# Cache attention: where the halves of the score rows are added, on VectorE or on TensorE

## What is computed

```python
qf = q.astype(jnp.float32) * (HEAD_DIM ** -0.5)
for k, _, kp in segs:
    s = jnp.einsum('bthjd,bshjd->bhjts', qf, k.astype(jnp.float32))
    dist = (q_pos[:, None] - kp[None, :]).astype(jnp.float32)
    s = jnp.where(dist >= 0, s - slopes[None, :, None, None, None] * dist, NEG_INF)
    scores.append(s)
p = jax.nn.softmax(jnp.concatenate(scores, axis=-1), axis=-1)
a = p[:, :, 0] - lam * p[:, :, 1]
...
    out = out + jnp.einsum('bhts,bshe->bthe', a[..., off:off + n], v.astype(jnp.float32))
```

## Time and profile before

| | |
|---|---|
| median of 3 runs | 3715.0 us (3714.81 to 3717.43) |
| span of the profiled execution | 3713.6 us |
| PE busy | 3481.8 us, 94% |
| DVE busy | 1857.9 us, 50% |
| ACT busy | 1495.0 us, 40% |
| POOL busy | 609.4 us, 16%, none of it before slice 6 of the 40 |
| first stage of the key pages | about 470 to 558 us |
| seven passes | 568 to 1349 us |

### The profile page before, as it was taken

One profiled execution on the slowest core, in us unless ns is written; L12 is line 12 of the kernel. 1 busy time (PEld: TensorE's weight loads), 2 busy tenths in 40 slices (PEclk: granted clock), 3 DMA queues, 4 the chain that ended last, 5 costly groups with the idle time before them and its releaser, 6 DMA issues.

```text
span 3713.6 us, 65939 instructions
## 1 busy us (share of the span) xinstructions
PE 3481.8 (94%) x24423; PEld 3386.7 (91%) x24423; DVE 1857.9 (50%) x2599; ACT 1495.0 (40%) x2255; POOL 609.4 (16%) x489
## 2 busy tenths in 40 slices
PE   5999979999999987899999999999889999999997
PEld 5999978888898885789999999999889999999997
DVE  4333366666666677454444444444564444444444
ACT  3232147777777775333222222222333333333223
POOL 0000007777777740000000000000000000000000
PEclk8999999999999998799999999999999999999998
DMA  4344357777887781234444444444334444444442
GB/s 144 124 154 134 128 176 290 292 292 292 303 315 292 292 305 61 68 125 136 140 144 137 143 141 137 148 137 144 120 102 149 158 141 156 148 148 148 148 150 71
DMA packets 337733, 634.25 MB, mean 171 GB/s; under 512 B 10056, under 2 KB 255919, under 8 KB 303151
## 3 DMA queue, kind: packets, MB, share of 16 engines
q1 hardware_dynamic: 335042, 616.60, 47.9%
q0 software_dynamic: 2192, 14.25, 1.2%
q10 hardware_dynamic: 348, 1.07, 0.1%
HBM read 623.11 MB, written 9.23 MB: 170 GB/s over the span
## 4 chain that ended last, share of the span: by engine, by line
PE 89%; DVE 5%; issue 2%; ACT 2%; DMA 0%; POOL 0%; DVEq 0%; ACTq 0%; POOLq 0%
PE ps L1436 66%; PE ps L1542 6%; PE ps L1530 6%; PE ps L1557 5%; PE ps L1568 2%; DVE halves L1055 1%; PE ps L1572 1%; ACT halves L666 1%; PE ps L1797 1%; ACT halves L696 1%; DVE parts L928 0%; PE ps L1696 0%; DMA io_tm<-in_x_sample_dram 0%; DVE xf L954 0%; DVE halves L1066 0%
## 5 line engine op out<-in xcount | busy, mean ns | idle before, releaser
L1436 PE MATMUL ps<-xhi,halves 128*128 128x336 f32 (+1 forms) x6784 | 1551.7, 314 | 28.4 <-DVE xlo L960 14.4
L901 DVE TENSOR_TENSOR halves<-raw,halves 128x2048 fp32r<-128x2048 f32 x328 | 751.8, 2292 | 1000.5 <-ACT halves L605 1000.5
L1436 PEld LDWEIGHTS ps<-xhi,halves 128*128 128x128 f32 x6784 | 1156.7, 189 | 32.6 <-issue 32.5
L605 ACT ACTIVATE halves<-raw 128x2048 fp32r<-128x2048 f32 x331 | 633.8, 1915 | 1200.1 <-PE ps L1436 1186.0
L1436 PE MATMUL ps<-xlo,halves 128*128 128x336 f32 (+1 forms) x3392 | 1066.7, 314 | 0.0
L1436 PEld LDWEIGHTS ps<-xlo,halves 128*128 128x128 f32 x3392 | 642.1, 189 | 0.0
L545 POOL TENSOR_TENSOR halves<-raw,halves 128x512 fp32r<-128x512 f32 x452 | 575.1, 1311 | 313.2 <-ACT halves L696 313.1
L1055 DVE TENSOR_TENSOR halves<-ps,halves 128x512 fp32r<-128x512 f32 x512 | 341.5, 688 | 194.2 <-ACT halves L666 194.1
L666 ACT ACTIVATE halves<-ps 128x512 fp32r<-128x512 f32 x512 | 292.1, 594 | 225.7 <-PE ps L1530 225.4
L1436 PE MATMUL ps<-hA_hi,halves 128*128 128x336 f32 (+1 forms) x1408 | 374.8, 313 | 4.9 <-DVE hB_lo L1328 4.9
L1436 PE MATMUL ps<-hB_hi,halves 128*128 128x336 f32 (+1 forms) x1408 | 373.7, 312 | 0.0
(11 more groups left out here) (178 smaller groups left out, 2796.1 us busy)
## 6 DMA issues: line engine op xcount, KB each, us to landing
raw<-in_w_gate_up_dram SPq DMA_DIRECT2D x176, 1024.0 KB, 5.1
raw<-in_cache_k_dram SPq DMA_DIRECT2D x128, 1024.0 KB, 4.8
raw<-in_cache_v_dram SPq DMA_DIRECT2D x128, 1024.0 KB, 4.9
raw<-in_w_down_dram SPq DMA_DIRECT2D x88, 1024.0 KB, 5.0
raw<-in_w_qkv_dram SPq DMA_DIRECT2D x48, 1024.0 KB, 5.1
raw<-in_w_o_dram SPq DMA_DIRECT2D x16, 1024.0 KB, 5.7
out_dram<-kv_tm POOLq DMA_DIRECT2D x4, 1024.0 KB, 5.4
raw<-in_w_pool_dram SPq DMA_DIRECT2D x4, 1024.0 KB, 5.1
```

The costliest lines, as they stand in the source:

```text
L605: act.activation(whi[t][:, :], raw[r][:, :], ACT.Copy).then_inc(hi_ready[t], 1)
L901: dve.tensor_tensor(wlo[t][:, :], raw[r][:, :], whi[t][:, :].bitcast(F32), ALU.subtract)\
L1436: mm = pe.matmul(out, l, r, start=first and n == 0, stop=last and n == 2)
```

## The change

The fold matmuls go. `turn_bank` becomes `turn_probs`, which transposes probabilities only. `raw_scores` becomes four reductions on VectorE over 64 partitions each, two that stay in their half and two that read one half and write the other, so that `s_raw[:, 0, :]` and `s_raw[:, 1, :]` hold the two rows of each score. For that the two parts of the queries change places for g = 1 (`qp_at`). `scores_out` adds the bias to the first and then the second to it, both in SBUF, with a wait on VectorE's own semaphore between (`score_bias`), and does not wait for ScalarE any more. Bank 3 is used less often, and so its counts change.

```diff
@@ def qp_at
-            at = 8 * P * g + TS * half_
+            at = 8 * P * g + TS * ((half_ + g) % 2)
@@ VectorE
                 two = ps[2][:, :].rearrange("p (g a k) -> p g k a", g=2, a=2)
-                dve.tensor_reduce(s_raw[:, :, :], two, AX.X, ALU.add).then_inc(bank_free[2], 1)
-
-            def scores_out(p, fill, last):
-
-                dve.wait_ge(bank_full[3], before("cache", 3, True) + fill + 1)
-                ins = dve.scalar_tensor_tensor(out=sc[:, bass.ds(PAGE * p, PAGE)], in0=alibi,
-                                               scalar=pagestep[:, bass.ds(p, 1)], in1=ps[3][:, P:P + PAGE],
-                                               op0=ALU.add, op1=ALU.add)
-                ins.then_inc(bank_free[3] if last else score_step, 1)
+                halves_ = (slice(0, TS), slice(TS, P))
+                for g in range(2):
+                    dve.tensor_reduce(s_raw[halves_[g], 0, :], two[halves_[g], g], AX.X, ALU.add)\
+                        .then_inc(score_parts, 1)
+                dve.tensor_reduce(s_raw[halves_[0], 1, :], two[halves_[1], 0], AX.X, ALU.add).then_inc(score_parts, 1)
+                dve.tensor_reduce(s_raw[halves_[1], 1, :], two[halves_[0], 1], AX.X, ALU.add).then_inc(bank_free[2], 1)
+
+            def scores_out(p, page):
+
+                dve.wait_ge(score_parts, 3 * page + 3)
+                dve.wait_ge(bank_free[2], bank_n("cache", 2, 0) + page + 1)
+                dve.scalar_tensor_tensor(out=s_raw[:, 0, :], in0=alibi, scalar=pagestep[:, bass.ds(p, 1)],
+                                         in1=s_raw[:, 0, :], op0=ALU.add, op1=ALU.add).then_inc(score_bias, 1)
+                dve.wait_ge(score_bias, page + 1)
+                dve.tensor_tensor(sc[:, bass.ds(PAGE * p, PAGE)], s_raw[:, 0, :], s_raw[:, 1, :], ALU.add)\
+                    .then_inc(score_step, 1)
@@ VectorE, step of a pass
                         if v == 1 or not first:
-                            dve.wait_ge(a_hi, (NPAGE + 1) * s + m + 2)
-                            scores_out(m - 1, CF0 + CFS * s + m + 1, False)
+                            scores_out(m - 1, NPAGE + NPAGE * s + m - 1)
@@ TensorE
-            def turn_bank(fill, page, count, slot):
-
+            def turn_probs(fill, count, slot):
 
                 pe.wait_ge(bank_free[3], before("cache", 3, False) + fill + 1)
-                if page is not None:
-                    pe.wait_ge(bank_free[2], bank_n("cache", 2, 0) + page + 1)
-                    for g in range(2):
-                        mm = pe.matmul(ps[3][:, P:2 * P], fold[:, TS * (1 - g):TS * (1 - g) + P], s_raw[:, g, :],
-                                       start=(g == 0), stop=(g == 1))
-                if count is not None:
-                    pe.wait_ge(staged, count)
-                    mm = pe.matmul(ps[3][:, 0:H * NT], stage[slot][:, :], comb, start=True, stop=True)
-                mm.then_inc(bank_full[3], 1)
+                pe.wait_ge(staged, count)
+                pe.matmul(ps[3][:, 0:H * NT], stage[slot][:, :], comb, start=True, stop=True).then_inc(bank_full[3], 1)
+
+            def scores_free(page):
+
+                pe.wait_ge(score_parts, 3 * page)
+                pe.wait_ge(bank_free[2], bank_n("cache", 2, 0) + page)
```

More of the change, by code:

```diff
@@ L69 @@
 U_END = U_F1 + 12 * BLOCKS
-CF0, CFS = NPAGE, NPAGE + 2
+CF0, CFS = 0, NPAGE + 1
 FREE_USES = [
@@ L336, in trunk @@
         v_hi, v_part, v_used = map(sem, ("v_hi", "v_part", "v_used"))
+        score_parts, score_bias = map(sem, ("score_parts", "score_bias"))
         best_step, smax, sexp, csum, score_step, c_ready, staged, a_hi, anew_ready, dve_step = map(
@@ L1096, in _ @@
                     if j > 0:
-                        scores_out(4 * i + j - 1, 4 * i + j - 1, True)
-                        dve.wait_ge(bank_free[3], bank_n("cache", 3, j) + 4 * i)
+                        scores_out(4 * i + j - 1, 4 * i + j - 1)
+                        dve.wait_ge(score_step, 4 * i + j)
                         best_of(4 * i + j, 4 * i + j - 1)
                 raw_scores(U_C0 + 3, i, 4)
-                scores_out(4 * i + 3, 4 * i + 3, True)
-                dve.wait_ge(bank_free[3], bank_n("cache", 3, 4) + 4 * i)
+                scores_out(4 * i + 3, 4 * i + 3)
+                dve.wait_ge(score_step, 4 * i + 4)
                 best_of(4 * i + 4, 4 * i + 3)
@@ L1115, in softmax @@
                 dve.wait_ge(best_step, NPAGE + 1 + (NPAGE - 1) * s)
-                dve.wait_ge(bank_free[3], bank_n("cache", 3, CF0 - 1) + 1 + CFS * s)
+                dve.wait_ge(score_step, NPAGE + NPAGE * s)
                 dve.tensor_reduce(mx, sc[:, LASTP:], AX.X, ALU.max).then_inc(csum, 1)
@@ L1144, in new_part @@
                 dve.wait_ge(anew_ready, s + 1)
-            dve.wait_ge(bank_free[3], bank_n("cache", 3, CF0 - 1) + 1)
             new_scores(0)
@@ L1177, in _ @@
                 raw_scores(U_CM + 3, s * (NPAGE // 2) + NPAGE // 2 - 1, 4)
-                scores_out(NPAGE - 1, CF0 + CFS * s + NPAGE + 1, True)
+                scores_out(NPAGE - 1, NPAGE + NPAGE * s + NPAGE - 1)
                 softmax(s + 1)
@@ L1590, in _ @@
                     turn(p, U_C0 + j, 2, i, 4)
-                    if j > 0:
-                        turn_bank(p - 1, p - 1, None, 0)
-                    else:
-                        pe.wait_ge(bank_free[2], bank_n("cache", 2, 0) + p)
-                    turn(p, U_C0 + j, 3, i, 4)
+                    turn(p, U_C0 + j, 3, i, 4)
+                    if j == 0:
+                        pe.wait_ge(bank_free[2], bank_n("cache", 2, 0) + p)
+                    else:
+                        scores_free(p)
                     for g in range(4):
@@ L1599, in _ @@
                             turn(p + 1, U_C0 + j + 1, g - 2, i, 4)
-                turn_bank(p, p, None, 0)
             A1 = NPAGE + 1
@@ L1605, in _ @@
                     turn(NPAGE + NPAGE * s, U_CM + 1, g, s * (NPAGE // 2), 4)
-                turn_bank(CF0 + CFS * s, None, A1 * s + 1, 0)
+                turn_probs(CF0 + CFS * s, A1 * s + 1, 0)
                 def two_steps(i):
@@ L1625, in two_steps @@
                         skip = first and v == 0
-                        turn_bank(CF0 + CFS * s + m + 1, None if skip else page - 1, A1 * s + m + 2, (v + 1) % 2)
+                        turn_probs(CF0 + CFS * s + m + 1, A1 * s + m + 2, (v + 1) % 2)
+                        scores_free(page)
                         if skip:
@@ L1634, in _ @@
                     two_steps(i)
-                turn_bank(CF0 + CFS * s + NPAGE + 1, NPAGE * (s + 2) - 1, None, 0)
             s = NB - 1
-            turn_bank(CF0 + CFS * s, None, A1 * s + 1, 0)
+            turn_probs(CF0 + CFS * s, A1 * s + 1, 0)
             with pe.Fori(0, NPAGE // 4) as i:
@@ L1641, in _ @@
                     pe.wait_ge(bank_free[3], B3 + CF0 + CFS * s + m + 2)
-                    turn_bank(CF0 + CFS * s + m + 1, None, A1 * s + m + 2, (v + 1) % 2)
+                    turn_probs(CF0 + CFS * s + m + 1, A1 * s + m + 2, (v + 1) % 2)
                     for g in range(4):
```

2 lines of the change are left out of this document (1 added, 1 removed).

## The result

The changed kernel takes 3871.2 us, median of 4 runs (3869.81 to 3875.15), beside 3715.2 of the kernel before on the same chip: ratio 1.042, interval 1.0405 to 1.0434. The direction was forecast; the size was not: + 156 us and not + 49, well outside the range. The profiled execution spans 3870.5 us, 156.9 more than before. TensorE's share of the chain that ended last fell from 89% to 71%, VectorE's rose from 5% to 13%, and time in which nothing was waited for ("issue") from 2% to 10%.

The account below looks back on a forecast made before the run. A loop through TensorE and VectorE was taken to set each cache-attention step; + 36 us in seven passes and + 13 in the first stage gave + 49, a 3764 us median. Range 3735 to 3800, forecast's chance 0.60.

Parts of the forecast that it names:

- The loop of TensorE and VectorE: Cache attention passes: one loop through both engines sets each step, 1.07 + 0.74 + 4.67 = 6.48 us.
- four pieces: Passes' step: reduction to split 1.72, split to third transpose group 0.74, group to fourth split 2.33, then to reduction 1.94.
- The fold's 0.45: TensorE's fold matmuls, on the path in fourteen steps of each pass: removing them alone would save 44 us.
- Half the partitions save nothing: VectorE's new reductions: 256 elements take 0.42 us each, over 64 partitions as over 128.
- The four reductions: Ahead of the first key split: 0.43 us apart without overlap, 1.72 in place of 1.07, 0.65 later per step.
- The upper bound, 0.46: Largest distance between reductions, from an instruction behind its own semaphore; with it the total is about + 64 us.
- what is added behind the last key split: VectorE's bias add, row add and maximum behind the fourth split: they cost a step 0.05 us on average.
- Rival 2: VectorE's tail becomes the bound: three SBUF instructions each 0.20 longer, + 88 us in all or 3803; chance 0.14.
- rest: Passes, besides fold and reductions: tail + 0.05 us a step, and 1.0 more at each pass's end.
- First stage, + 13: Sixteen key pages in four groups: reductions add 1.11 three times a group, a group 3.16, four 12.6, the end 0.5.
- The wait of 2.3: First stage: TensorE's wait behind VectorE's key split grows from 1.18 to 2.3 us.

Follow-up runs that it names:

- experiment 6: Kernel before, with the second of its two fold matmuls and the scores of g = 1 left out: 3691.4 us, ratio 0.9927.
- experiments 4 and 3: Changed kernel: 4, four reductions over all 128 partitions, addition across halves left out, 3803.1 us; 3, one input of each add in PSUM, all arithmetic kept, 3807.3 us.
- experiment 2: Kernel before, with GpSimd's low part of the value pages computed over 16 of each 512 columns: 3713.5 us, ratio 0.9993.
- experiment 1: Changed kernel, with GpSimd's low part of the value pages computed over 16 of each 512 columns: 3781.7 us, ratio 1.0175.
- experiment 9: Changed kernel, with four unused fp32 matmuls added per first-stage page while TensorE waits for VectorE: 3865.6 us, ratio 1.0396.

## Why the prediction was wrong

**Right.** The loop of TensorE and VectorE that sets the step, and its division: three of four pieces came out within 0.09. The fold's 0.45 was worth its full price, as far as leaving out half of it tells (experiment 6). Half the partitions save nothing.

**The four reductions** were sized at 0.43 apart and are 0.455, so 1.81 and not 1.72: 0.09 x 105 = 9 us. The upper bound, 0.46 from the row of an instruction behind a semaphore, was the nearer one. That a change of partitions takes the overlap away, cited there from the Trainium skill, is borne out by experiments 4 and 3: 0.335 without it.

**The failed step: "what is added behind the last key split", + 0.05.** It measured + 0.94: from K to the reduction it is 2.83 in the mean, where the kernel before has 2.34 and without the fold 1.89, and where the sum had 1.94. The add was priced at 0.29 from the maximum's row, and that same instruction took 0.49 in every second step. The sum took the lower value for the new adds. Rival 2 had the place and the sign, but priced it at 0.20 for each of three, "for a cause that the row doesn't name", and argued against it from the steps where it took 0.29. The cause could have been read from the trace of the kernel before: GpSimd's row stood beside it, and the copy of 80 columns at 1.27 us (experiment 2) lay just ahead of the rows. 0.20 was the chance remainder of one GpSimd instruction; the new add waits for most of one. In the trace the bias add gets its turn between two of them, then VectorE waits 0.16 for its own semaphore, and the next GpSimd instruction is already running. That this wait gives the turn away is read from the rows; no run took the wait alone out.

| seven passes, us | predicted | measured |
|---|---|---|
| fold gone | - 44 | - 42 (2 x 21 in experiment 6) |
| reductions | + 68 | + 78 (105 x 0.74) |
| stall on GpSimd | 0 | + 90 (experiment 1) |
| rest | + 12 | + 9 |
| sum | + 36 | + 135 |

The measured parts are taken from different kernels and need not simply add. The rest holds pass ends and, new, 0.25 us of "issue" ahead of every second reduction, 10.7 us in 42 times, which idle time used to cover. It stands where the loop turns; that the loop's branch is its cause is not shown.

**First stage, + 13 and got + 26.3.** The prediction's own terms with 1.81 give 12 x 1.20 for the reductions, + 1.9 for group and stage ends, - 2.1 for the fold: 14. Its last page meets GpSimd, which has begun on the first values (the prediction had GpSimd idle in this stage); VectorE, first stage's end:

```profile
580.69 1.40 DVE L1086 SCALAR_TENSOR_TENSOR s_raw<-cst,s_raw 128x128 f32<-128x128 f32 x1
582.24 1.13 DVE L1089 TENSOR_TENSOR sc<-s_raw 128x128 f32 x1
583.40 1.23 DVE L1095 TENSOR_TENSOR sc<-sc 128x128 f32<-128x128 f32 x1
584.56 0.87 DVE L1077 TENSOR_REDUCE s_raw<-ps 64x128 f32<-64x256 f32 x2
```

From bias add to reduction that is 3.87 us where 573.82 to 575.05 is 1.23: some 2.6. About 10 are left, and 10 is what the changed kernel's seven long pages come to (counted in experiment 9). The wait of 2.3 was forecast (2.40 came), but the sum held TensorE's durations fixed. What falls of the clock when a wait recurs in every page was the missing term.

## What to carry to other kernels

Before an addition is moved to VectorE, list where both its inputs lie and what GpSimd runs at that time: with two SBUF inputs it cost here its own time and the rest of GpSimd's instruction; with one of the two in PSUM it cost its own time only. A row that takes two different times for the same work may point at a shared resource; find it before taking the lower value, above all when the change puts such instructions where no idle time stands behind them. Lengthening a wait of TensorE can cost more than the wait, where it recurs in each turn of a loop.

## What the runs showed of the chip that I had not expected

A VectorE add of 128 x 128 takes 0.29 us alone and up to 1.26 beside GpSimd instructions of 1.3 us, ending about 0.15 behind one of them; with one input in PSUM it takes 0.29 in all 128 instances. A copy with a single SBUF input and an SBUF output (80 columns) was held as well, 1.27 against 0.20. The Trainium skill, SBUF — State Buffer, section "Who interferes with whom", names copies and `tensor_scalar` as able to contend with GpSimd in their two-port modes. The trace agrees on the stall; the mode it doesn't show. Reductions are 0.335 us apart over 128 partitions and 0.455 where the partitions change. TensorE's granted clock was 0.87 to 0.91 with a wait of 2.40 us in each page, 0.96 with 1.46 and 1.00 with 1.18.
